# A compression layer with its token windows as the stationary operand: two column halves of TensorE, the sums turned afterwards, and one query moved between the two layers

## The chip, the cores and the metric

The kernel runs on one core of one Trainium2 chip. The metric is device microseconds (us) of that core for one launch. Five engines work side by side, each through its own list of instructions in order: TensorE (PE, with its weight loads PEld), VectorE (DVE), ScalarE (ACT), GpSimd (POOL) and SyncE (SP), which issues the loads from HBM. They wait for one another through semaphores.

## The reference

Two transformer blocks over 256 tokens of width 1024: a first model of two layers (four mixers, a dense and an expert feed-forward), then a second one (a recurrent layer, a feed-forward, a sparse attention layer, a feed-forward). The change touches the attention layer of the second model, in its preparation:

```python
def compress(t, pos_emb, w1, b1, w2, b2):
    n_cmp = (S - CMP_BLOCK) // CMP_STRIDE + 1          # 15
    idx = jnp.arange(n_cmp)[:, None] * CMP_STRIDE + jnp.arange(CMP_BLOCK)[None, :]
    blocks = t[:, idx] + pos_emb[:, None, :]
    blocks = blocks.transpose(0, 1, 3, 2, 4).reshape(B, n_cmp, N_KV_GROUPS, CMP_BLOCK * HEAD_DIM)
    return jax.nn.gelu(blocks @ w1 + b1) @ w2 + b2

k_cmp = compress(k_c, cmp_pos[0], cmp_w1[0], ...)      # then rmsnorm and rope
v_cmp = compress(v_c, cmp_pos[1], cmp_w1[1], ...)
```

There are 15 blocks in each of 4 groups, so 60 rows. The first layer of each of the two compressions takes those 60 rows of 2048 numbers to 256 hidden numbers. The queries of the same attention layer are a projection from 1024 to 1024, cut here into four "queries" of 256 columns.

## The kernel before

All weights pass through one stream of units of 128 x 2048 fp32 numbers (1 MB), numbered in the order of `stages()`. SP loads unit after unit into a ring of four slots (`load`, L765); a slot's next load waits until PE has used the unit that held it, which PE tells by the counter `unit_used`. In the stages around the change the slots follow one another in turn, so unit n + 4 waits for unit n. A "raw" unit is multiplied as it stands, in fp32: each such product is two passes (two matmul records) of PE. Every other unit is split first: ACT copies it rounded (`split`, `high<-ring`, L832), DVE subtracts that from the unit (`low`, `ring_lo<-ring,high`, L2434), and PE makes three single-pass products of the parts (`split_mm`). PE's products all go through the helper line L1409, ACT's instructions through L832.

The stage `keys_and_queries` (L2245 on PE) does in this order: four tiles of keys and two of values, `k_mean`, query 0, query 1, `k_rot` (4 passes of 512 columns), `hidden_layer(0)`, `query_rot(0)` (4 such passes), `hidden_layer(1)`, query 2 with the gates woven in (`gate_step`), the second layer of the key compression (`k_cmp`), query 3 with means, `cmp_mean` and the value compression woven in (`mean_step`, `cmp_step`), `cmp_rot`. The attention follows.

`hidden_layer(v)` (L2167) takes two raw units `cmp`. The weights, 128 x 128 pieces of the unit in `ring`, are the stationary operand; the moving one is the 60 windows in `work` at EXW. Two column tiles m of the hidden layer, each a sum over 16 pieces: 32 products, 64 passes. The result stands with hidden numbers in the partitions, so ACT can add the bias of each hidden number and take the gelu as it evicts (`hidden_layer`, L1323). ACT loads a table before the first gelu. `gate_step` writes the bank from which gelu 0 reads, and so waits for it.

On ACT the order is: eviction of queries 0 and 1, gelu 0, split of the unit of query 2, gelu 1, split of the unit of query 3, `k_copies` (8 copies), eviction of query 2, `k_cmp`, gates, `cmp_norm`. On DVE: the rotation of the keys `k_rope` (L2685 to L2687), `low` of query 2's unit, `query_rope(0)` (the same three lines), `low` of query 3's unit, `cmp_squares`, `cmp_normed`.

Of the kernel before, what the change touches and what calls it, by code (L numbers as in the profile page):

```python
# [25 lines left out]
ACT = mybir.ActivationFunctionType  # L26
AX = mybir.AxisListType.X

P = 128
# [48 lines left out]
def stages():  # L78

    def mixers(l):  # L80
        return [(f"win{l}", NWIN, False), (f"gate_a{l}", 8, False), (f"branch_a{l}", 2, True),
                (f"gate_b{l}", 8, False), (f"branch_b{l}", 2, True), (f"out{l}", NPROJ, False)]

    return [*mixers(0), ("dense", 2 * PART_UNITS, False), *mixers(1), ("moe", NE * PART_UNITS, False),
            ("lru_in", 6, False), ("lru_gate", 1, True), ("lru_last", 2, False), ("out2", NPROJ, True), ("f0", 2 * PART_UNITS, False),
            ("kv", 6, False), ("query_a", 2, False), ("cmp", 4, True), ("query_b", 2, False),
            ("out3", NPROJ, False), ("f1", 2 * PART_UNITS, False)]


# [199 lines left out]
def weight_stream(a):  # L289
# [12 lines left out]
    def narrow(w):  # L302
        for n in range(0, w.shape[1], 256):
            add(rows(w[:, n:n + 256]))
# [55 lines left out]
    for v in range(2):  # L360
        for i in range(2):
            add(rows(a["cmp_w1_2"][v][1024 * i:1024 * i + 1024]))
    narrow(a["b_w_in_2"][0][:, D // 2:D])
    output(a["b_w_out_2"][0])
    ffn(1)
    return np.stack(units)
# [47 lines left out]
def build(nc, stream, consts_in, params_in, x_in, out):  # L414
    units = Units()
    assert units.count == stream.shape[0]
    with ExitStack() as ctx:
# [3 lines left out]
        def sem(name):  # L421
            return ctx.enter_context(nc.semaphore(name))
# [138 lines left out]
        Y_AT, Z_IN, R_AT, GI_AT, A_AT, XR_AT, TH_AT = 0, 2048, 8192, 10240, 12288, 18944, 20992  # L561
        Q_BANK = (6, 7, 4, 5)

        def q_means(i):
            return banks[:, 6 + i, 0:32]

# [45 lines left out]
        def slots_of(a):  # L612
# [27 lines left out]
        kv_out = sem("kv_out")  # L640
        KV_V = Steps(sem("kv_vector"), "windows", "k_squares", "k_normed", "k_rope", "cmp_squares", "cmp_normed",
                     "cmp_rope", "v_cmp")
        KV_P = Steps(sem("kv_products"), "k_mean", "k_rot", "k_cmp", "cmp_mean", "v_cmp", "cmp_rot")
        KV_A = Steps(sem("kv_scalar"), "k_norm", "hidden0", "hidden1", "k_copies", "k_cmp", "cmp_norm")

        Q_P = Steps(sem("q_products"), "rot0", "gates", "mean0", "rot1", "mean1")
        Q_A = Steps(sem("q_scalar"), "input", "out0", "out1", "out2", "gates", "norm0", "out3", "norm1")
# [179 lines left out]
        def _(act):  # L827
# [3 lines left out]
            def f(out_, in_, func, **kw):  # L831
                return act.activation(out_, in_, func, **kw)  # L832
# [442 lines left out]
            def keys_and_queries():  # L1275
# [21 lines left out]
                run(f(w(KSQ, 1024), bank(2, 2), ACT.Sqrt, bias=const("rms_eps")), KV_A, "k_norm")  # L1297
                query(0)
                query(1)
                hidden_layer(0)  # L1300
                split(units.at("query_b"))
                hidden_layer(1)
                split(units.at("query_b", 1))
                act.wait_ge(KV_V.sem, KV_V.at("k_rope"))
                for b in range(2):
                    for d in range(2):
# [3 lines left out]
                query(2)  # L1310
                act.wait_ge(KV_P.sem, KV_P.at("k_cmp"))
                run(f(w(KCM, G * NC), bank(2)[:, 0:G * NC], ACT.Identity, bias=par("cmp_b2k")), KV_A, "k_cmp")
                act.wait_ge(Q_P.sem, Q_P.at("gates"))
                run(f(w(GA, 96), bank(0)[:, 0:96], ACT.Sigmoid), Q_A, "gates")
                act.wait_ge(KV_P.sem, KV_P.at("cmp_mean"))
# [5 lines left out]
                    split(units.at("out3", i))  # L1321

            def hidden_layer(v):  # L1323
                act.wait_ge(unit_used, units.at("cmp", 2 * v + 1) + 1)
                for m in range(2):
                    ins = f(w(HIDN + 128 * v + 64 * m, G * NC), bank(v)[:, 64 * m:64 * m + G * NC],
                            ACT.Gelu_apprx_tanh, bias=par("cmp_b1", 2 * v + m))
                run(ins, KV_A, f"hidden{v}")

            def query_unit(q):  # L1330
                return units.at("query_a", q) if q < 2 else units.at("query_b", q - 2)

            def query(q):
                act.wait_ge(unit_used, query_unit(q) + 1)
                f(w(QSQ + 512 * q, 512), banks[:, Q_BANK[q], :], ACT.Square)
                run(f(w(QR + 512 * q, 512), banks[:, Q_BANK[q], :], ACT.Copy, scale=par("q_norm")), Q_A, f"out{q}")
# [70 lines left out]
        def _(pe):  # L1407
# [758 lines left out]

            def hidden_layer(v):  # L2167

                first = units.at("cmp", 2 * v)
                for i in range(2):  # L2170
                    raw_ready(first + i)
                if v == 0:
                    pe.wait_ge(KV_V.sem, KV_V.at("windows"))
                for m in range(2):
                    for j in range(CB // 2):
                        ins = mm(bank(v)[:, 64 * m:64 * m + G * NC], raw_rows(first + j // 8, 8)[:, j % 8, m * P:m * P + P],
                                 w(EXW + 960 * v + j * G * NC, G * NC), j == 0, j == CB // 2 - 1)
                ins.then_inc(unit_used, 2)

            def query(q):  # L2180

                pe.wait_ge(kv_out, 4 if q < 2 else 6)
                if q == 0:
                    pe.wait_ge(Q_V.sem, Q_V.at("input_lo"))
                g = units.at("query_a", q) if q < 2 else units.at("query_b", q - 2)
                split_ready(g)
                for j in range(2):
                    for k in range(KT):
                        if q == 2:
                            gate_step(KT * j + k)  # L2190
                        elif q == 3:
                            mean_step(0, KT * j + k)
                            cmp_step(KT * j + k)
                        ins = split_mm(banks[:, Q_BANK[q], j * T:j * T + T], parts_of(g, 2 * P * k + j * P, P),
                                       [v[:, k, :] for v in LOWER], k == 0, k == KT - 1)
                ins.then_inc(unit_used, 1)
# [27 lines left out]
            def cmp_step(n):  # L2224

                if n == 4 * TT:
                    pe.wait_ge(KV_V.sem, KV_V.at("cmp_squares"))
                    KV_P.mark(mm(bank(1)[:, 0:G * NC], const("head_mean"), w(EXW, G * NC)), "cmp_mean")
                g = n - 4 * TT - 1
                if 0 <= g < G:  # L2230
                    at, _ = CONSTS["ones"]
                    o = bank(3, rows=slice(0, NC))[:, g * HD:g * HD + HD]
                    for m in range(2):
                        mm(o, w(HIDN + 128 + 64 * m + g * NC, NC), par("cmp_w2v", m * HD, HD), m == 0, False)
                    ins = mm(o, consts[0:1, at:at + NC], par("cmp_b2v", 0, HD, slice(0, 1)), False, True)
                    if g == G - 1:
                        KV_P.mark(ins, "v_cmp")

# [6 lines left out]
            def keys_and_queries():  # L2245
# [14 lines left out]
                KV_P.mark(ins, "k_rot")  # L2260
                hidden_layer(0)
                query_rot(0)
                hidden_layer(1)
                query(2)
                pe.wait_ge(KV_A.sem, KV_A.at("hidden1"))
                pe.wait_ge(KV_V.sem, KV_V.at("k_rope"))
                for m in range(2):
                    ins = mm(bank(2)[:, 0:G * NC], par("cmp_w2k", m * P, P), w(HIDN + 64 * m, G * NC), m == 0, m == 1)
                KV_P.mark(ins, "k_cmp")
                query(3)  # L2270
                pe.wait_ge(KV_V.sem, KV_V.at("cmp_normed"))
                KV_P.mark(mm(bank(2)[:, 0:G * NC], const("swap"), w(KCM, G * NC)), "cmp_rot")
# [144 lines left out]
        def _(dve):  # L2417
# [769 lines left out]
            def keys_and_queries():  # L3187
# [33 lines left out]
                       KV_V, "k_rope")  # L3221
                low(units.at("query_b"))
                query_rope(0)
                low(units.at("query_b", 1))
                dve.wait_ge(KV_A.sem, KV_A.at("k_cmp"))
                k, sq = w(KCM, G * NC), w(EXW, G * NC)
                run(tt(sq, k, k, MUL), KV_V, "cmp_squares")
# [139 lines left out]
```

## Time and profile before

| | |
|---|---|
| median of 3 runs | 1875.35 us (1872.57 to 1876.69) |
| profiled execution: its own time, its span | 1869.12 us, 1867.3 us |
| PE busy, share of the span | 1818.3 us, 97% |
| DVE, ACT busy | 1403.9 us (75%), 1019.7 us (55%) |
| HBM read | 360.39 MB, 194 GB/s over the span |

The profile is of one execution; its span is what the trace covers, and its own time is 1.8 us longer. Starts in the rows are microseconds from the start of the span. A busy PE is not always PE at its peak: its records overlap, so the pace of a stream is read from the distance of starts.

### The profile page before, as it was taken

How to read it: one execution, taken by the hardware profiler on the slowest of the kernel's cores; microseconds unless marked ns; L12 is line 12 of the kernel's file. 1: busy time of each engine (PE TensorE's matmuls, PEld its weight loads, DVE VectorE, ACT ScalarE, POOL GpSimd, SP SyncE). 2: the span in 40 equal slices, each digit the busy share in tenths (PEclk: the TensorE clock that was granted, in tenths of full speed). 3: DMA queues.
4: the chain of work that ended last, by engine and by line, in shares of the span. 5: the costliest groups of instructions: out<-in, count | busy, mean ns of one | idle time of the engine just before them, and what ended most of it. 6: DMA issues, size and time to landing. Idle time of an engine off the chain costs nothing.

```text
span 1867.3 us, 30106 instructions
## 1 busy us (share of the span) xinstructions
PE 1818.3 (97%) x12742; PEld 1577.1 (84%) x12742; DVE 1403.9 (75%) x1540; ACT 1019.7 (55%) x1209; POOL 148.7 (8%) x161
## 2 busy tenths in 40 slices
PE   7999999999999999999999999999999999799999
PEld 7998898888899889788888888895888898578887
DVE  5988667856588966699999999775857564958674
ACT  5663346433566425477777777766533435855431
POOL 0021000201002100000000000000112000001110
PEclk9999999999999999999999999999999999899999
DMA  7432345553443234589999999555553343016451
GB/s 275 158 106 100 113 181 228 186 196 123 168 160 114 92 113 181 194 333 353 350 353 371 350 349 351 192 176 203 188 194 144 143 162 136 1 70 248 169 218 63
DMA packets 52267, 364.49 MB, mean 195 GB/s; under 512 B 5920, under 2 KB 6048, under 8 KB 9760
## 3 DMA queue, kind: packets, MB, share of 16 engines
q1 hardware_dynamic: 50832, 357.79, 51.5%
q0 software_dynamic: 1296, 4.72, 0.7%
q8 instruction: 103, 1.69, 0.4%
q14 instruction: 36, 0.29, 0.0%
HBM read 360.39 MB, written 2.10 MB: 194 GB/s over the span
## 4 chain that ended last, share of the span: by engine, by line
PE 59%; DVE 4%; ACT 2%; issue 1%; DVEq 0%; ACTq 0%
PE banks L1409 57%; ACT work L832 1%; DVE work L3254 1%; DVE small L3258 1%; PE banks L2070 1%; ACT h_parts L832 0%; DVE h_parts L2491 0%; PE banks L2016 0%; PE banks L2316 0%; DVE work L2816 0%; DVE work L2813 0%; DVE more_lo L2434 0%; PE banks L1456 0%; ACT L832 0%; ACT more_high L832 0%
## 5 line engine op out<-in xcount | busy, mean ns | idle before, releaser
L1409 PE MATMUL banks<-h_parts,high 128*128 128x256 f32 (+1 forms) x2576 | 554.0, 307 | 3.3 <-DVE h_parts L2491 2.5
L1409 PE MATMUL banks<-h_parts,ring_lo 128*128 128x256 f32 x1664 | 469.3, 282 | 0.0
L1409 PEld LDWEIGHTS banks<-h_parts,high 128*128 128x128 f32 x2576 | 417.3, 191 | 32.3 <-issue 10.6
L2434 DVE TENSOR_TENSOR ring_lo<-ring,high 128x2048 fp32r<-128x2048 f32 x154 | 352.8, 2299 | 70.1 <-ACT high L832 68.2
L832 ACT ACTIVATE high<-ring 128x2048 fp32r<-128x2048 f32 x154 | 292.4, 1904 | 72.2 <-DMA ring<-weights_in 66.0
L1409 PEld LDWEIGHTS banks<-h_parts,ring_lo 128*128 128x128 f32 x1664 | 317.5, 191 | 0.1
L832 ACT ACTIVATE work<-banks 128x512 f32<-128x512 f32 (+5 forms) x135 | 86.6, 647 | 254.8 <-PE banks L1409 246.9
L2434 DVE TENSOR_TENSOR more_lo<-more,more_high 128x2048 fp32r<-128x2048 f32 (+1 forms) x86 | 188.6, 2203 | 31.9 <-ACT more_high L832 31.8
L1409 PE MATMUL banks<-h_parts,more_high 128*128 128x512 f32 x592 | 207.6, 394 | 2.0 <-DVE more_lo L2434 1.5
L832 ACT ACTIVATE more_high<-more 128x2048 fp32r<-128x2048 f32 (+1 forms) x86 | 158.0, 1842 | 61.7 <-DMA more<-weights_in 61.5
L832 ACT ACTIVATE glu<-scr 128x256 f32<-128x256 f32 x66 | 27.6, 419 | 219.9 <-DVE scr L2458 219.9
L1409 PE MATMUL banks<-more_high,h_parts 128*128 128x512 f32 (+1 forms) x440 | 138.1, 384 | 0.1
L2455 DVE TENSOR_REDUCE scr<-banks 128x512 f32<-128x1024 f32 x66 | 80.8, 1224 | 75.2 <-PE banks L1409 75.2
L1409 PE MATMUL banks<-high,h_parts 128*128 128x256 f32 (+1 forms) x520 | 135.9, 343 | 0.0
L1409 PEld LDWEIGHTS banks<-h_parts,more_high 128*128 128x128 f32 x592 | 111.1, 188 | 27.8 <-DVE more_lo L2434 2.1
L2434 DVE TENSOR_TENSOR ring_lo<-ring,more_high 128x2048 fp32r<-128x2048 f32 (+1 forms) x60 | 133.5, 2226 | 0.2
L1409 PE MATMUL banks<-h_parts,more_lo 128*128 128x256 f32 x448 | 125.2, 280 | 0.0
L832 ACT ACTIVATE more_high<-ring 128x2048 fp32r<-128x2048 f32 (+1 forms) x60 | 111.3, 1856 | 24.3 <-DMA ring<-weights_in 24.2
L1409 PE MATMUL banks<-work 32*32 32x32 f32 (+8 forms) x2592 | 119.0, 237 | 5.1 <-DVE work L2743 2.4
L1409 PE MATMUL banks<-more_high,g_hi 128*128 128x512 f32 x294 | 115.9, 394 | 0.0
L1409 PEld LDWEIGHTS banks<-work 32*32 32x32 f32 (+5 forms) x2592 | 94.1, 132 | 25.3 <-issue 15.4
L1409 PE MATMUL banks<-more_high,g_lo 128*128 128x512 f32 x294 | 115.0, 391 | 0.0
(283 smaller groups left out, 3076.4 us busy)
## 6 DMA issues: line engine op xcount, KB each, us to landing
ring<-weights_in SPq DMA_DIRECT2D x225, 1024.0 KB, 4.9
more<-weights_in SPq DMA_DIRECT2D x104, 1024.0 KB, 5.2
more<-weights_in SPq DMA_DIRECT2D x8, 512.0 KB, 4.0
ring<-weights_in SPq DMA_DIRECT2D x6, 512.0 KB, 3.8
consts<-consts_in SPq DMA_DIRECT2D x1, 2034.0 KB, 17.4
params<-params_in SPq DMA_DIRECT2D x1, 1162.5 KB, 11.1
x<-x_in SPq DMA_DIRECT2D x2, 512.0 KB, 4.1
normed_rows<-scr POOLq DMA_DIRECT2D x2, 512.0 KB, 10.3
```

The costliest lines, as they stand in the source:

```text
L832: return act.activation(out_, in_, func, **kw)
L1409: return pe.matmul(out_, lhsT, rhs, start=start, stop=stop, **kw)
L2070: ins = pe.transpose(bank(2 + s % 2)[:, c * P:c * P + P], token_hidden[:, s % 2, c * P:c * P + P], const("ident"))
L2434: tt(lo_of(g), ring_of(g), hi_of(g).bitcast(F32), SUB).then_inc(unit_lo, 1)
L2455: chain.to(dve.tensor_reduce(ffn_sum(t), pair, AX, ADD), sums_made, done)
L3254: ins = tt(s[:, 2 * r:2 * r + 2, :], grid(bank(2 * (k % 2) + r)[:, 0:2 * n], 2), bc(mask, 2), ADD)
L3258: run(dve.tensor_reduce(least, s, AX, MAX, negate=True))
```

## The change

The first layer is turned round: the 60 windows become the stationary operand and the 128 x 128 weight pieces the moving one. The two tiles m are written to partitions 0 to 59 and 64 to 123 of one bank, in turn, so each uses one half of PE's columns. The sums now stand with windows in the partitions; ACT copies them to `work`, PE turns them with two transposes (`hidden_turn`), and ACT takes the gelu as before. The stage list becomes cmp0, query_b (query 2), cmp1, query_c (query 3): the first layer of the values and its turn come behind query 2 and `k_cmp`, the turn inside query 3. `unit_used` is now raised after each unit of the layer, not by two at its end.

```diff
-            ("kv", 6, False), ("query_a", 2, False), ("cmp", 4, True), ("query_b", 2, False),
+            ("kv", 6, False), ("query_a", 2, False), ("cmp0", 2, True), ("query_b", 1, False),
+            ("cmp1", 2, True), ("query_c", 1, False),
...
# ACT, keys_and_queries
                 query(0)
                 query(1)
+                split(units.at("query_b"))
                 hidden_layer(0)
-                split(units.at("query_b"))
-                hidden_layer(1)
-                split(units.at("query_b", 1))
                 act.wait_ge(KV_V.sem, KV_V.at("k_rope"))
...
                 query(2)
                 act.wait_ge(KV_P.sem, KV_P.at("k_cmp"))
                 run(f(w(KCM, G * NC), bank(2)[:, 0:G * NC], ACT.Identity, bias=par("cmp_b2k")), KV_A, "k_cmp")
+                split(units.at("query_c"))
+                hidden_layer(1)
...
             def hidden_layer(v):
-                act.wait_ge(unit_used, units.at("cmp", 2 * v + 1) + 1)
+                act.wait_ge(unit_used, units.at(f"cmp{v}", 1) + 1)
                 for m in range(2):
-                    ins = f(w(HIDN + 128 * v + 64 * m, G * NC), bank(v)[:, 64 * m:64 * m + G * NC],
+                    ins = f(w(EXW + 960 * v, P, rows=window_rows(m)), bank(v, rows=window_rows(m))[:, 0:P], ACT.Copy)
+                run(ins, KV_A, f"sums{v}")
+                act.wait_ge(KV_P.sem, KV_P.at(f"turned{v}"))
+                for m in range(2):
+                    ins = f(w(HIDN + 128 * v + 64 * m, G * NC), bank((v + m) % 2)[:, P + 64 * m:P + 64 * m + G * NC],
                             ACT.Gelu_apprx_tanh, bias=par("cmp_b1", 2 * v + m))
# PE
             def hidden_layer(v):
-                first = units.at("cmp", 2 * v)
-                for i in range(2):
-                    raw_ready(first + i)
+                first = units.at(f"cmp{v}")
                 if v == 0:
                     pe.wait_ge(KV_V.sem, KV_V.at("windows"))
+                for j in range(CB // 2):
+                    if j % 8 == 0:
+                        raw_ready(first + j // 8)
+                    for m in range(2):
+                        ins = mm(bank(v, rows=window_rows(m))[:, 0:P], w(EXW + 960 * v + j * G * NC, G * NC),
+                                 raw_rows(first + j // 8, 8)[:, j % 8, m * P:m * P + P], j == 0, j == CB // 2 - 1)
+                    if j % 8 == 7:
+                        ins.then_inc(unit_used, 1)
+
+            def hidden_turn(v):
+
+                pe.wait_ge(KV_A.sem, KV_A.at(f"sums{v}"))
                 for m in range(2):
-                    for j in range(CB // 2):
-                        ins = mm(bank(v)[:, 64 * m:64 * m + G * NC], raw_rows(first + j // 8, 8)[:, j % 8, m * P:m * P + P],
-                                 w(EXW + 960 * v + j * G * NC, G * NC), j == 0, j == CB // 2 - 1)
-                ins.then_inc(unit_used, 2)
+                    ins = pe.transpose(bank((v + m) % 2)[:, P + 64 * m:P + 64 * m + G * NC], w(EXW + 960 * v, P, rows=window_rows(m)),
+                                       const("ident")[window_rows(m), 64 * m:64 * m + G * NC])
+                KV_P.mark(ins, f"turned{v}")
...
# PE, query(q)
                     for k in range(KT):
+                        if q == 3 and KT * j + k == 2:
+                            hidden_turn(1)
...
# PE, cmp_step
                 if n == 4 * TT:
+                    pe.wait_ge(KV_A.sem, KV_A.at("hidden1"))
...
# PE, keys_and_queries
                 hidden_layer(0)
                 query_rot(0)
-                hidden_layer(1)
+                hidden_turn(0)
                 query(2)
-                pe.wait_ge(KV_A.sem, KV_A.at("hidden1"))
                 pe.wait_ge(KV_V.sem, KV_V.at("k_rope"))
                 for m in range(2):
                     ins = mm(bank(2)[:, 0:G * NC], par("cmp_w2k", m * P, P), w(HIDN + 64 * m, G * NC), m == 0, m == 1)
                 KV_P.mark(ins, "k_cmp")
+                hidden_layer(1)
                 query(3)
```

What PE does from `k_rot` (the first row) to the first step of query 2, before (one row is one instruction of the program, xN of them):

```order
L1409 MATMUL banks<-work,consts 128x512 x2
L1409 MATMUL banks<-work,ring 128x60 x32
L1409 MATMUL banks<-work,consts 128x512 x2
L1409 MATMUL banks<-work,ring 128x60 x32
L1409 MATMUL banks<-params,work 128x48
L1409 MATMUL banks<-hb_hi,high 128x256
```

And in the changed kernel (`params,work 128x48` is the first gate step of query 2):

```order
L1420 MATMUL banks<-work,consts 128x512 x2
L1420 MATMUL banks<-ring,work 60x128 x32
L1420 MATMUL banks<-work,consts 128x512 x2
L2196 MATMUL banks<-consts,work 128x60 x2
L1420 MATMUL banks<-params,work 128x48
L1420 MATMUL banks<-hb_hi,high 128x256
```

The second layer has left this place, and the two transposes of the first one's sums stand directly ahead of query 2.

What ACT does from the eviction of query 1 on, before:

```order
L832 ACTIVATE work<-banks,params 128x512
L832 ACT_TABLE_LOAD
L832 ACTIVATE work<-banks,params 128x60 x2
L832 ACTIVATE high<-ring 128x2048
L832 ACTIVATE work<-banks,params 128x60 x2
L832 ACTIVATE high<-ring 128x2048
L832 ACTIVATE work<-work 64x2x256 x8
L832 ACTIVATE work<-banks 128x512
L832 ACTIVATE work<-banks,params 128x512
L832 ACTIVATE work<-banks,params 128x60
L832 ACT_TABLE_LOAD
```

And in the changed kernel:

```order
L839 ACTIVATE work<-banks,params 128x512
L839 ACTIVATE high<-ring 128x2048
L839 ACTIVATE work<-banks 60x128 x2
L839 ACT_TABLE_LOAD
L839 ACTIVATE work<-banks,params 128x60 x2
L839 ACTIVATE work<-work 64x2x256 x8
L839 ACTIVATE work<-banks 128x512
L839 ACTIVATE work<-banks,params 128x512
L839 ACTIVATE work<-banks,params 128x60
L839 ACTIVATE high<-ring 128x2048
L839 ACTIVATE work<-banks 60x128 x2
L839 ACTIVATE work<-banks,params 128x60 x2
```

The split of query 2's unit (the first `high<-ring`) moved ahead of the first gelu, which now has two copies and the transposes ahead of it, with its table load behind the wait for the transposes. The split of query 3's unit (the second `high<-ring`) moved from ahead of the eight copies of `k_copies` to behind the eviction of query 2 and `k_cmp`.

DVE and SP have the same rows in the same order as before; the units that they take are renumbered.

## Rows read from the trace of the kernel before

**Rows 1.** The page: busy time of engines, and the clock that PE was granted.

```profile
PE 1818.3 (97%) x12742; PEld 1577.1 (84%) x12742; DVE 1403.9 (75%) x1540; ACT 1019.7 (55%) x1209; POOL 148.7 (8%) x161
...
PEclk9999999999999999999999999999999999899999
```

**Rows 2.** Timeline of PE around the layers: start, duration, operation, passes, idle before.

```profile
1532.00 1.88 PE L1409 MATMUL banks<-work,consts 128*128 128x512 f32 x4
1533.71 7.25 PE L1409 MATMUL banks<-work,ring 128*128 128x60 f32 x64
1540.80 1.94 PE L1409 MATMUL banks<-work,consts 128*128 128x512 f32 x4
1542.58 7.25 PE L1409 MATMUL banks<-work,ring 128*128 128x60 f32 x64
1550.25 0.39 PE L1409 MATMUL banks<-params,work 128*128 128x48 f32 x2 [0.42 <-issue]
...
1560.48 0.55 PE L1409 MATMUL banks<-work,params 128*128 128x60 f32 x4
1560.87 0.34 PE L1409 MATMUL banks<-consts,work 128*128 128x2 f32 x2
...
1571.56 0.33 PE L1409 MATMUL banks<-work,consts 128*128 128x60 f32 x2
```

**Rows 3.** Weight loads of PE, 1515 to 1572, then 1572 to 1660, by form.

```profile
L1409 PEld LDWEIGHTS banks<-work,ring 128*128 128x128 f32 x128 | 14.6, 192 | 1.0 <-issue 1.0
...
L1409 PEld LDWEIGHTS banks<-work 128*64 128x64 f32 x192 | 10.8, 143 | 2.9 <-issue 2.9
```

**Rows 4.** Timeline of PE in the attention: transposes, sums in two column halves.

```profile
1638.48 0.63 PE L2316 MATMUL banks<-consts,work 128*128 128x128 f32 x4 [0.61 <-ACT work L832]
1639.04 2.85 PE L1409 MATMUL banks<-work 15*64 15x128 f32 x40
1641.81 0.61 PE L2310 MATMUL banks<-consts,work 128*15 128x128 f32 x4
...
1645.07 1.09 PE L2316 MATMUL banks<-consts,work 128*128 128x128 f32 x8 [2.03 <-ACT work L832]
1646.09 3.20 PE L1409 MATMUL banks<-work 15*64 15x128 f32 x24
```

**Rows 5.** Windows in that stream: length, busy and passes touched per engine, clock.

```profile
1639.55:1639.65 0.10, 0.10 (x4) 0.10 (x4) 0.10 (x1) 0.10 (x1) 0.00 (x0) 1.00 0.00 0
1639.55:1640.20 0.65, 0.65 (x14) 0.65 (x14) 0.61 (x2) 0.65 (x3) 0.00 (x0) 1.00 0.00 0
```

**Rows 6.** Timeline of ACT, first a norm's evictions, then this stage.

```profile
1480.10 4.22 ACT L832 ACTIVATE h_parts<-banks,params 128x128 fp32r<-128x128 f32 x16
...
1532.75 0.68 ACT L832 ACTIVATE work<-banks,params 128x512 f32<-128x512 f32 x1
1541.05 1.28 ACT L832 ACT_TABLE_LOAD   x1 [7.61 <-PE banks L1409]
1542.34 0.51 ACT L832 ACTIVATE work<-banks,params 128x60 f32<-128x60 f32 x2
1545.84 1.91 ACT L832 ACTIVATE high<-ring 128x2048 fp32r<-128x2048 f32 x1 [2.99 <-issue]
...
1552.23 5.11 ACT L832 ACTIVATE work<-work 64x512 f32<-64x512 f32 x8
1560.74 0.60 ACT L832 ACTIVATE work<-banks 128x512 f32<-128x512 f32 x1 [3.40 <-PE banks L1409]
1561.35 1.03 ACT L832 ACTIVATE work<-banks,params 128x512 f32<-128x512 f32 x2
...
1565.97 1.28 ACT L832 ACT_TABLE_LOAD   x1 [2.03 <-PE banks L1409]
```

**Rows 7.** Timeline of DVE in this stage.

```profile
1533.98 1.22 DVE L2685 TENSOR_TENSOR work<-banks,consts 128x1024 f32<-128x1024 f32 x1 [4.09 <-PE banks L1409]
...
1536.50 1.23 DVE L2687 TENSOR_TENSOR work<-work 128x1024 f32<-128x1024 f32 x1
1547.86 2.29 DVE L2434 TENSOR_TENSOR ring_lo<-ring,high 128x2048 fp32r<-128x2048 f32 x1 [10.13 <-ACT high L832]
...
1568.24 0.28 DVE L3230 SCALAR_TENSOR_TENSOR work<-work,params 128x60 f32<-128x60 f32 x1
```

**Rows 8.** SP's loads L765, 1525 to 1545: issues and time to landing.

```profile
L765 SPq DMA_DIRECT2D ring<-weights_in x4: 328/328/431, 1526.4 to 1541.4; - x4
...
DMA to landing us min/median/max: 4.8/4.8/6.9
```

**Rows 9.** Windows of all engines (PE first, then PEld, DVE, ACT, POOL), clock.

```profile
1578.10:1605.30 27.20, 17.80 (x110) 14.09 (x110) 23.88 (x55) 20.14 (x52) 0.00 (x0) 0.50 0.00 1
...
1643.10:1645.00 1.90, 0.00 (x0) 0.00 (x0) 1.61 (x5) 1.90 (x7) 0.00 (x0) 1.00 0.00 0
1646.40:1653.10 6.70, 6.70 (x40) 5.14 (x37) 5.21 (x4) 4.11 (x5) 0.00 (x0) 0.50 0.00 1
1258.60:1260.20 1.60, 0.00 (x0) 0.00 (x0) 1.57 (x3) 1.55 (x4) 0.00 (x0) 1.00 0.64 102
1261.00:1270.00 9.00, 9.00 (x24) 4.37 (x23) 3.27 (x4) 8.18 (x14) 0.00 (x0) 1.00 0.18 76
```

More of the change, by code:

```diff
@@ L362, in weight_stream @@
             add(rows(a["cmp_w1_2"][v][1024 * i:1024 * i + 1024]))
-    narrow(a["b_w_in_2"][0][:, D // 2:D])
+        narrow(a["b_w_in_2"][0][:, D // 2 + 256 * v:D // 2 + 256 * v + 256])
     output(a["b_w_out_2"][0])
@@ L562, in build, with window_rows @@
         Q_BANK = (6, 7, 4, 5)
+        def window_rows(m):
+            return slice(64 * m, 64 * m + G * NC)
         def q_means(i):
@@ L642, in build @@
                      "cmp_rope", "v_cmp")
-        KV_P = Steps(sem("kv_products"), "k_mean", "k_rot", "k_cmp", "cmp_mean", "v_cmp", "cmp_rot")
-        KV_A = Steps(sem("kv_scalar"), "k_norm", "hidden0", "hidden1", "k_copies", "k_cmp", "cmp_norm")
+        KV_P = Steps(sem("kv_products"), "k_mean", "k_rot", "turned0", "k_cmp", "turned1", "cmp_mean", "v_cmp", "cmp_rot")
+        KV_A = Steps(sem("kv_scalar"), "k_norm", "sums0", "hidden0", "k_copies", "k_cmp", "sums1", "hidden1",
+                     "cmp_norm")
         Q_P = Steps(sem("q_products"), "rot0", "gates", "mean0", "rot1", "mean1")
@@ L1330, in query_unit @@
             def query_unit(q):
-                return units.at("query_a", q) if q < 2 else units.at("query_b", q - 2)
+                return units.at("query_a", q) if q < 2 else units.at(("query_b", "query_c")[q - 2])
             def query(q):
@@ L2184, in query @@
                     pe.wait_ge(Q_V.sem, Q_V.at("input_lo"))
-                g = units.at("query_a", q) if q < 2 else units.at("query_b", q - 2)
+                g = units.at("query_a", q) if q < 2 else units.at(("query_b", "query_c")[q - 2])
                 split_ready(g)
@@ L3223, in keys_and_queries @@
                 query_rope(0)
-                low(units.at("query_b", 1))
+                low(units.at("query_c"))
                 dve.wait_ge(KV_A.sem, KV_A.at("k_cmp"))
```

## The prediction

> **What bounds the kernel now.** The page comes first [rows 1]. PE is busy for 1818.3 of 1867.3 us, 97%, and at the full granted clock but for one slice of forty. So a microsecond less of PE work is a microsecond less of time, as long as PE doesn't wait in its place. The second view is PE's timeline around the two layers [rows 2]. Each layer is 64 passes of 60 moving columns. The first lasts from 1533.71 to 1540.80, 7.09 us or 111 ns a pass; the second from 1542.58, with a tail and a wait of 0.42 us, to query 2 at 1550.25: 7.67 us. Between them stand the four passes of `query_rot(0)`, and the four of `k_rot` with the same shape take 1.71 us (1532.00 to 1533.71). A 512-column fp32 pass thus has a pace of 427 ns, or 0.83 ns a column; 60 columns would be 50 ns. The layer's 111 ns are therefore not the moving columns, and the other thing that each pass has is a full load of 128 x 128 weights [rows 3].
>
> **The layer turned round.** The trace holds the same form in the attention: `at_sum` multiplies with 64 stationary columns, 128 moving ones, and its two results go to partitions 0 to 63 and 64 to 127 in turn. One such block of 40 passes goes from 1639.04 to 1641.81, 69 ns a pass [rows 4]. In its inside a window of 0.10 us touches 4 passes and one that is 0.55 us longer touches 14: 55 ns a pass [rows 5]. By the pace above a pass of 128 columns alone would be 107 ns, so the two halves run together. The stationary load of 64 columns shows 143 ns against 192 for 128 [rows 3]. I take 55 ns, since the layer is one unbroken alternation of 64 passes: 3.5 us. 69 ns is the dearer neighbour (4.4 us). The far end is that nothing is gained by the halves, 111 ns as today.
>
> What lies between 55 and 69 is the change of form: 40 passes at 55 ns are 2.2 us, and the other 0.57 us falls on five changes between stationary pieces of 15 and 128 rows and into and out of the block, 0.11 us each. That is what I put beside every change here: into and out of the layer 0.22 us, so 3.72 us for a layer. The Trainium skill (TensorEngine Tiling (Array Packing), Tiling Modes) has the rule that speaks against this change: changing the tiling mode, not just the tile, drains TensorE. The trace agrees, with 0.11 us a change; that rule without a price would leave the layer at 3.5 us.
>
> **From the first layer to query 2.** Before: 1533.71 to 1550.25, 16.54 us [rows 2]. After: layer 3.72, `query_rot(0)` 1.71, transposes. Four transposes of `at_turn` stand 0.56 us apart from the next work (1638.48 to 1639.04) [rows 4], so two cost 0.28 us, with a change 0.39. Sum 5.82 us, at 1539.5. The copies of the sums on ACT are covered: ACT starts 0.26 us after PE goes on (1560.48, 1560.74), and 16 evictions of 128 columns took 4.22 us, 0.26 each [rows 2, 6], so they are done at 1537.4 + 0.26 + 0.53 = 1538.2, a little under 1 us before `query_rot(0)` ends. Without that cover they would cost 0.8 us.
>
> The gelu isn't covered. Query 2 begins with a gate step into the bank from which the gelu reads. Before, ACT did its table load and two gelus (1541.05 to 1542.85, 1.80 us) [rows 6] while PE worked on the second layer; that layer has now gone behind query 2. So PE waits for 0.26 us to reach ACT, 1.80 us, and about 0.07 us back: **2.13 us** of new wait. Query 2 starts 5.82 + 2.13 = 7.95 us after the layer's start, at 1541.7, against 16.54: a lead of 8.6 us. The wait of 0.42 us is in this lead. Its cause was the load of query 2's unit, issued when the first layer had freed its slot (SP's last issue of this stretch is at 1541.4 [rows 8]), then ACT's split at 1545.84 and DVE's `low` until 1550.15 [rows 6, 7]. Now that unit takes the slot that query 0 frees: issue at 1526.4, landing 4.8 to 6.9 us later, by 1533.3 [rows 8]. ACT splits it after query 1's eviction (done 1533.4), DVE takes its low part after `k_rope` (done 1537.7) [rows 6, 7], so it is there at 1540.1, 1.6 us ahead. Cmp1's units come into slots freed at 1532 and halfway through the first layer, and query 3's at its end: all are in the ring by 1545, before use.
>
> **From query 2 to query 3.** Query 2 itself stays 10.23 us (1550.25 to 1560.48), and I count from its end, T = 1551.9. Before, query 3 began at T + 0.39, behind `k_cmp` [rows 2]. Now PE does `k_cmp` and the second layer, 0.39 + 3.72 = 4.1 us. But the split of query 3's unit was moved on ACT behind the eviction of query 2 and `k_cmp`. That chain: 0.26 us to ACT, eviction with `k_cmp` 1.64 (1560.74 to 1562.38), split 1.92, 0.1 to DVE, `low` 2.29, 0.1 to PE [rows 6, 7]: T + 6.31. So PE waits **2.2 us** more, with its second layer hidden inside the chain whatever its price up to 5.9 us. ACT meanwhile stands idle for some 5 us between `k_copies` (5.11 us, done near 1546.9) and T + 0.26; the queue order alone keeps the split out of there. The loss against T + 0.39 is 5.92 us.
>
> **In query 3.** Two transposes with two changes: 0.28 + 0.22 = 0.50 us. The second layer's gelu has no table load and must be done at step 8 of 16, some 3 us later. The table loads for gates and `cmp_norm` and the DVE work follow `cmp_mean` in that step. Before, they ended at 1568.5 (from ACT's 1565.97), 3 us ahead of `cmp_rot` at 1571.56 [rows 2, 6, 7], and that distance stays. Nothing is late next; the attention starts when query 3 ends.
>
> **The sum.** 8.6 - 5.92 - 0.50 = 2.2 us less. Counted the other way: 7.09 + 7.67 go; 2 x 3.72 + 0.39 + 0.50 + 2.13 + 2.2 = 12.66 come; 2.1 us. The profiled execution has a span of 1867.3 us and its own time of 1869.12, so this one would be near 1866.9. It lies 6.2 us under the median of 1875.35, for no reason that a row shows, and I take the difference to the median: **1873.1 us**, 0.12% less. A measurement of this kernel tells a difference from about 0.2%, 3.8 us; most of the saving of 6.9 us on the layers is spent on two waits.
>
> **Rivals.**
> - *The halves are dearer than in `at_sum`.* At 69 ns a pass the first layer is 0.7 to 0.9 us longer and the second stays hidden: gain 1.4, 1873.9. At 111 ns the first costs 3.6 more and the second ends at T + 7.7, 1.4 after the chain: 2.8 us slower, 1878.2. For it: 60 columns are not 64, and the moving side comes from the ring. Against it: load, columns and alternation are the same form. Chance 0.10, nearly all of it within 0.2%.
> - *The clock falls in the new waits.* PE was held at 0.50 for 27.3 us from 1578.1, and for 6.8 us after the idle time of 2.03 us at 1643.04 and eight transposes [rows 4, 9]. There 24 passes of the halves took 3.13 us, 130 ns each instead of 69 [rows 4]. The changed kernel has waits of 2.1 and 2.2 us, one just behind transposes. Against it: around the 1.70 us of idle time at 1258.5, between dense work, the clock stayed at 1.00 [rows 9], and here too dense products lie on both sides. A stretch of 6.8 us at half the clock costs 3.4 us: one makes 1876.5, one behind each wait 1879.9, slower by 4.6 us. It decides above 12 us at the low clock in this stage. Chance 0.15, about half of it slower by over 0.2%.
> - *The attention's slow stretch moves.* It runs at 1.2 GHz for 27.3 us with PE busy for 17.8 of 27.2 [rows 9]. If it begins later or ends earlier by a quarter, that is 17.8 / 4 / 2 = 2.2 us, and with the gain of the layers 4.4: 1870.9. It can go the other way as well. Chance 0.15.
> - *The waits don't show*, because gate steps or the split are let through earlier than the order has them: up to 2.2 + 4.3 = 6.5 us, 1868.8. Against it: both waits are semaphores that the moved instructions raise. Chance 0.05.
>
> **How the numbers follow.** My forecast, a gain of 1 to 3.5 us, has 0.55. Range 1868.8 to 1878.6: from the last rival, through the spread of the shown runs (1872.6 to 1876.7, shifted by 2.2), to between one and two stretches at the low clock; its two ends leave some 0.1 each. Faster by over 0.2%: most of the third and fourth rivals and the forecast's edge, 0.23. Slower: 0.11. Within: 0.66.
>
> **What would show it.** In the changed profile the 64 passes of a layer, 60 stationary and 128 moving columns, go by in 3.5 to 3.8 us; PE has an idle time of about 2.1 us ahead of query 2, ended by ACT's gelu, and one of about 2.2 us ahead of query 3, ended by DVE's `low`; ACT is idle for 5 us between `k_copies` and the eviction of query 2; from the start of the first layer to `cmp_rot` 35.6 us pass, before 37.85. I am wrong if the first layer has a pace near 70 or 110 ns, if either wait is missing or longer, or if the granted clock falls between 1539 and 1570.

## The result, and the profile after

| | before | changed |
|---|---|---|
| median of 6 runs each | 1873.96 us (1870.96 to 1876.69) | 1880.76 us (1870.71 to 1883.69) |
| the profiled execution | 1869.12 us | 1870.71 us |
| its mean granted clock | 0.991 | 0.989 |

The ratio is 1.0038, with a 95% interval of 1.002 to 1.0057: slower by a little, 6.8 us at the medians. The forecast was 1873.1 us in a range to 1878.6. The profile of the changed kernel is of its fastest execution; the other five took 1878.8 to 1883.7 us at a mean clock of 0.981 to 0.984.

PE's timeline shows every planned piece at nearly its planned size (start, duration, passes, idle before; compare [rows 2]):

```profile
1534.14 3.71 PE L1420 MATMUL banks<-ring,work 128*60 128x128 f32 x64
1537.78 1.98 PE L1420 MATMUL banks<-work,consts 128*128 128x512 f32 x4
1539.70 0.27 PE L2196 MATMUL banks<-consts,work 60*128 60x60 f32 x2
1542.01 0.39 PE L1420 MATMUL banks<-params,work 128*128 128x48 f32 x2 [2.04 <-ACT work L839]
...
1552.24 0.55 PE L1420 MATMUL banks<-work,params 128*128 128x60 f32 x4
1552.72 3.71 PE L1420 MATMUL banks<-ring,work 128*60 128x128 f32 x64
1558.58 0.35 PE L1420 MATMUL banks<-consts,work 128*128 128x2 f32 x2 [2.15 <-issue]
...
1575.98 0.52 PE L1420 MATMUL banks<-work,consts 128*128 128x60 f32 x2
```

A layer takes 3.64 us from start to start (3.72 forecast), 57 ns a pass; query 2 begins 7.87 us after the layer (7.95), behind an idle time of 2.04 us (2.13); query 3 begins 6.34 us after query 2's end (6.31), behind 2.15 us (2.2). At query 3's start the changed kernel is 2.7 us ahead, counted from the first layer. Then query 3 takes 17.4 us to `cmp_rot` at 1575.98, where 11.2 were forecast. ACT's timeline has the cause of the second wait, the split behind 5.48 us of idle time and query 2's eviction; DVE's `low` hangs on that split:

```profile
1541.90 5.12 ACT L839 ACTIVATE work<-work 64x512 f32<-64x512 f32 x8
1552.50 0.60 ACT L839 ACTIVATE work<-banks 128x512 f32<-128x512 f32 x1 [5.48 <-PE banks L1420]
1553.11 1.03 ACT L839 ACTIVATE work<-banks,params 128x512 f32<-128x512 f32 x2
1554.17 1.91 ACT L839 ACTIVATE high<-ring 128x2048 fp32r<-128x2048 f32 x1
...
1556.18 2.29 DVE L2457 TENSOR_TENSOR ring_lo<-ring,high 128x2048 fp32r<-128x2048 f32 x1 [12.14 <-ACT high L839]
```

The view puts PE's second wait down to "issue", but `low` ends at 1558.47, 0.11 us before query 3 starts, so it is what PE waited for.

Why query 3 is slow stands in the windows (engines as in [rows 9], the granted clock behind POOL):

```profile
1558.60:1561.00 2.40, 2.40 (x20) 2.20 (x21) 0.01 (x1) 0.71 (x3) 0.00 (x0) 1.00 0.96 294
1561.10:1578.10 17.00, 17.00 (x84) 14.19 (x84) 2.60 (x9) 4.29 (x7) 0.00 (x0) 0.50 0.12 41
1578.20:1588.30 10.10, 9.31 (x108) 7.86 (x106) 9.41 (x16) 6.64 (x5) 0.00 (x0) 1.00 0.22 91
1588.50:1608.80 20.30, 9.62 (x46) 6.66 (x48) 18.43 (x46) 15.20 (x51) 0.00 (x0) 0.50 0.01 1
```

About 2.5 us into query 3 the clock falls from 2.4 to 1.2 GHz and stays there for 17 us with PE busy all the time. It then comes back for 10 us, just for the part of the attention that ran at the low clock before. These are PE's rows there, two of the kernel before (L1409, L2316) and two of the changed one:

```profile
1576.64 10.28 PE L1409 MATMUL banks<-work 64*128 64x128 f32 x88
1592.04 1.11 PE L2316 MATMUL banks<-consts,work 128*128 128x128 f32 x4 [5.12 <-DVE work L3271]
...
1581.44 6.07 PE L1420 MATMUL banks<-work 64*128 64x128 f32 x88
1594.90 1.11 PE L2339 MATMUL banks<-consts,work 128*128 128x128 f32 x4 [7.39 <-DVE work L3294]
```

The 88 passes take 6.1 us instead of 10.3, but PE then waits 2.3 us longer for DVE, so from `cmp_rot` to these transposes only 1.6 us are won (18.92 against 20.48). Another 1.3 us come back near 1650, where the low stretch lasts 3.4 us instead of 6.8. So of the 4.0 us that the stage is longer (41.84 against 37.85) the attention gives back 2.9 in this execution. The 10 us at the full clock stand in all four profiles with a long fall in query 3 (below), so they aren't what makes this execution the fastest of its kernel; what the slower ones do differently this profile can't show.

### The profile page after: what moved, and what is told of

Its sections match the earlier page's. It is cut to its first block, busy times and chain, and to the rows that moved or that the text cites. A ratio compares the mean times of both kernels' runs of the same rounds, so it can differ in the third digit from the quotient of the medians.

```text
span 1868.9 us, 30119 instructions
## 1 busy us (share of the span) xinstructions
PE 1814.0 (97%) x12746; PEld 1570.7 (84%) x12746; DVE 1403.6 (75%) x1540; ACT 1020.7 (55%) x1213; POOL 148.9 (8%) x161
## 4 chain that ended last, share of the span: by engine, by line
PE 58%; DVE 5%; ACT 2%; issue 1%; DVEq 0%; ACTq 0%
PE banks L1420 57%; DVE work L3277 1%; DVE small L3281 1%; ACT work L839 1%; PE banks L2081 1%; ACT h_parts L839 0%; DVE h_parts L2514 0%; PE banks L2027 0%; DVE work L2839 0%; PE banks L2339 0%; DVE work L2836 0%; DVE more_lo L2457 0%; DVE ring_lo L2457 0%; ACT L839 0%; PE banks L1467 0%
## 5 line engine op out<-in xcount | busy, mean ns | idle before, releaser
L839 ACT ACTIVATE work<-banks 128x512 f32<-128x512 f32 (+6 forms) x139 | 87.8, 637 | 259.7 <-PE banks L1420 252.5
L1420 PE MATMUL banks<-work 32*32 32x32 f32 (+8 forms) x2592 | 115.1, 233 | 5.0 <-DVE work L2766 2.7
## 6 DMA issues: line engine op xcount, KB each, us to landing
normed_rows<-scr POOLq DMA_DIRECT2D x2, 512.0 KB, 10.2
```

The costliest lines, as they stand in the source:

```text
L1420: return pe.matmul(out_, lhsT, rhs, start=start, stop=stop, **kw)
```

## The experiments

Each run lists the mean granted clock c of every execution. The time at the low clock (1.2 GHz, half of the full one) is then 2 x (1 - c) x time, good to some 2 us for the rounding of c. Through the executions of one kernel the time rises by 0.35 to 0.43 us for each microsecond at the low clock (straight lines through the three sets of the kernel before, and through 12 executions of the changed one), so a time less 0.39 times its low time is an estimate of what that execution would take at the full clock. The profile has the same price: query 3 loses 6.2 us in 17 at the low clock, 0.36 for each. The last two columns are medians over the executions. A difference in the last column hangs on the slope where the low times differ much: at 0.36 the changed kernel gains 0.9 us, at 0.43 it gains 2.6. The runs came in three groups, each with its own runs of the kernel before on the same chip.

| kernel | runs | median us | ratio to before (95%) | low clock, us | less 0.39 x low |
|---|---|---|---|---|---|
| before, group 1 | 35 | 1871.0 | | 37 | 1857 |
| changed again | 12 | 1879.0 | 1.0039 (1.0025 to 1.0052) | 58 | 1855.5 |
| both waits filled | 12 | 1870.2 | 0.9993 (0.9982 to 1.0004) | 39 | 1855 |
| second wait only | 12 | 1875.3 | 1.0016 (1.0002 to 1.0029) | 56 | 1854.5 |
| neither wait | 12 | 1866.6 | 0.9973 (0.9961 to 0.9985) | 41 | 1851 |
| before, group 2 | 31 | 1873.6 | | 41 | 1857.5 |
| before with a wait | 11 | 1879.9 | 1.003 (1.0013 to 1.0048) | 56 | 1859 |
| first wait only | 9 | 1868.2 | 0.9966 (0.9936 to 0.9996) | 41 | 1854 |
| new order, old form | 12 | 1871.5 | 0.9985 (0.9973 to 0.9996) | 37 | 1857 |
| new form, old order | 12 | 1871.8 | 0.9986 (0.9973 to 0.9999) | 49 | 1853.5 |
| before, group 3 | 30 | 1872.8 | | 39 | 1857 |
| means in the wait | 12 | 1870.3 | 0.9996 (0.9982 to 1.0011) | 45 | 1853 |
| second wait filled | 12 | 1870.2 | 0.9988 (0.9975 to 1.0) | 37 | 1855 |
| neither wait, again | 12 | 1864.5 | 0.9957 (0.9944 to 0.9971) | 32 | 1851 |
| the same, attention's gap filled | 7 | 1864.5 | 0.9957 (0.9941 to 0.9973) | 26 | 1853.5 |

### The changed kernel again

> The changed kernel once more, to see how its executions spread and whether their time goes with the time at the low clock. Theory 1 (the waits ahead of query 2 and query 3 let the clock fall, in most executions already ahead of query 3 or at query 2): executions with a mean clock near 0.983 take about 1880 us, those near 0.989 about 1871 us; the profile has a stretch at 0.50 that begins between 1543 and 1562. Theory 2 (the added time is something else, such as loads or the chip's other noise): times between 1871 and 1884 us without relation to the mean clock.

1879.0 us, 8 above the kernel before. The time goes with the clock: from 1872.5 us at 0.988 to 1883.7 at 0.981. The windows of its profile:

```profile
1541.70:1543.60 1.90, 0.00 (x0) 0.00 (x0) 1.87 (x3) 1.84 (x4) 0.00 (x0) 1.00 0.94 358
1545.30:1548.60 3.30, 3.30 (x17) 3.30 (x17) 0.40 (x1) 3.24 (x6) 0.00 (x0) 0.50 0.01 2
1548.70:1559.60 10.90, 10.90 (x124) 10.44 (x123) 0.18 (x1) 3.51 (x4) 0.00 (x0) 1.00 0.25 90
1559.70:1561.80 2.10, 0.00 (x0) 0.02 (x1) 2.10 (x2) 0.54 (x2) 0.00 (x0) 1.00 1.01 402
1562.40:1582.70 20.30, 20.30 (x100) 17.17 (x100) 2.39 (x9) 5.08 (x9) 0.00 (x0) 0.50 0.16 55
```

Both waits are followed by a fall here. The one behind the first wait lasts 3.4 us, the one behind the second over 20 us. Theory 1 holds; the spread is that of the clock. This execution is at 0.986, so the median one (0.984) isn't profiled either.

### Both waits filled

```diff
+                if q == 2:
+                    keep_busy(4, 4)
+                elif q == 3:
+                    keep_busy(5, 4)
                 split_ready(g)
```

`keep_busy(b, n)` makes n products of constants of 256 columns into bank b, here free until the query writes it.

> Each of the two waits is filled with 4 products of constants into a free bank (8 passes of 256 fp32 columns, about 1.7 us of the 2.0 and 2.2 us of idle time); nothing of them is used. The waits themselves stay. Theory 1 (idle time lets the clock fall): the clock stays at 1.00 until the attention, the stage takes about 35.6 us, the median is about 2 us under the kernel before, near 1872. Theory 2 (the form of the layer, 60 stationary columns in halves, is what lets the clock fall): as the changed kernel, near 1880, with a fall before 1562.

PE's timeline at the two places, and the windows from there:

```profile
1541.71 0.27 PE L2196 MATMUL banks<-consts,work 60*128 60x60 f32 x2
1541.91 2.00 PE L1420 MATMUL banks<-consts 128*128 128x256 f32 x8
...
1558.37 1.99 PE L1420 MATMUL banks<-consts 128*128 128x256 f32 x8
1560.54 0.38 PE L1420 MATMUL banks<-consts,work 128*128 128x2 f32 x2 [0.17 <-DVE ring_lo L2461]
```

```profile
1560.50:1571.50 11.00, 10.96 (x91) 9.37 (x92) 1.35 (x5) 3.91 (x7) 0.00 (x0) 1.00 0.33 122
```

Query 3 still begins at the same distance from query 2, and still waits for DVE, but it runs at the full clock. The stage takes 35.5 us (1536.15 to 1571.68), where the forecast had 35.6. The time is 8.8 us under the changed kernel, with the same order, layer form and waits. So what costs is that PE is idle in the waits, and the halves and transposes are cleared. The median is 1.8 us lower than expected, at the same low time as before.

### Second wait only, first wait only

The first wait is taken away by turning the first layer's sums into banks 5 and 1, which the gate steps don't touch, and by waiting for the gelu ahead of `k_cmp`:

```diff
+        TURNED = ((5, 1), (1, 0))
...
-                if n == 0:
-                    pe.wait_ge(KV_A.sem, KV_A.at("hidden0"))
...
                 query(2)
+                pe.wait_ge(KV_A.sem, KV_A.at("hidden0"))
```

> The turned sums of the first layer go to banks 5 and 1, so the gate steps need not wait for the gelu; the wait for it stands ahead of k_cmp. The first wait (2.04 us) is gone, the second stays. Theory 1 with either wait sufficient: the clock still falls behind the second, near 1561, the median between 1874 and 1880. If the first wait is the one that decides (or both are needed): about 4 us under before, near 1870. Query 2 starts about 2 us earlier either way.

1875.3 us. Query 2 begins after 0.56 us of idle time (it now waits for DVE's low part of its unit), the second wait is 2.15 us, and the clock falls behind it: 17 us at 0.50 from 1562.6 in the profile. The time at the low clock is 56 us, close to the changed kernel's 58. Eight of the 12 executions are at a mean clock of 0.984 to 0.986, four at 0.988 to 0.992.

The second wait is taken away by the place of one line on ACT:

```diff
                 run(ins, KV_A, "k_copies")
+                split(units.at("query_c"))
                 query(2)
...
-                split(units.at("query_c"))
                 hidden_layer(1)
```

> The changed kernel with the split of query 3's unit moved on ACT to directly behind k_copies: the second wait (2.15 us) goes, the first (2.04 us, ahead of query 2) stays. Together with the run that had only the second wait it shows which of the two costs the clock. Theory 1a (either wait alone is enough): time at the low clock near that of the run with the second wait alone, median near 1874. Theory 1b (the first wait costs at most a short stretch, as in the profile that showed 3.4 us behind it): the time is that of the sum, 4.4 us under before, 1867 to 1869.

1868.2 us, a ratio of 0.9966. The first wait stands in the profile with 2.04 us of idle time, and the clock is 1.00 from there to `cmp_rot`. Only one of nine executions was at a mean clock under 0.989 (0.982, 1881.7 us). Theory 1b: the loss at the low clock hangs on the second wait. The first one still costs time by itself: at an equal clock this kernel takes 3 us more than the one with neither wait (1854 against 1851), whose stage is 1.5 us shorter in the profiles (31.87 against 33.36).

### Only the second wait filled

> The changed kernel with only the second wait filled, by 4 products of constants (8 passes of 256 columns, 1.7 us). The first wait is left. If the second wait alone makes the loss: as with both filled, about 1 us under the kernel before, no additional time at the low clock. If the first matters too: between that and the changed kernel.

The edit is the second half of that of both fillings. 1870.2 us and 37 us at the low clock, as with both filled. Its profile has a fall of 3.4 us behind the first wait (the first window), and none behind the second until the attention:

```profile
1543.70:1546.90 3.20, 3.20 (x17) 3.20 (x16) 0.31 (x1) 3.14 (x6) 0.00 (x0) 0.50 0.01 3
1558.00:1577.50 19.50, 18.82 (x152) 15.43 (x152) 8.78 (x17) 6.63 (x13) 0.00 (x0) 1.00 0.44 164
```

So the first wait is followed by a short stretch in some executions (two of the five profiles that have this wait unfilled), too little to be seen in the median. Stretches of 3.4 us stand at places without such a wait too, near 675 us in three of the 14 profiles.

### The kernel before with a wait

```diff
                 KV_P.mark(ins, "k_cmp")
+                pe.wait_ge(KV_V.sem, KV_V.at("cmp_squares"))
                 query(3)
```

> The kernel before with one wait added: PE waits ahead of query 3 until DVE has made the squares of the compressed keys (about 1.9 us of idle time; nothing else is changed, no halves, no turns, old order). Theory 1 (idle time of about 2 us ahead of query 3 lets the clock fall, whatever the form of the layer): about 15 to 20 us more at the low clock than the kernel before in most executions, the median 1.9 + 6 to 8 us above it, near 1880. Theory 2 (the fall also needs what the changed kernel does around the wait, the halves or the transposes): only the wait itself, about 1.9 us, 1873.

PE's timeline and the windows behind it, of a kernel with the old form and the old order:

```profile
1564.32 0.55 PE L1409 MATMUL banks<-work,params 128*128 128x60 f32 x4
1566.53 0.38 PE L1409 MATMUL banks<-consts,work 128*128 128x2 f32 x2 [1.66 <-DVE work L3228]
```

```profile
1566.60:1568.80 2.20, 2.20 (x19) 2.20 (x20) 0.00 (x0) 1.17 (x2) 0.00 (x0) 1.00 0.88 372
1568.90:1585.80 16.90, 16.90 (x83) 13.86 (x83) 2.82 (x10) 3.04 (x5) 0.00 (x0) 0.50 0.05 13
```

An idle time of 1.66 us makes the kernel before 6.2 us slower, with 15 us more at the low clock; at an equal clock 1.5 to 2 us of this are left, which is the wait itself. So the fall comes without anything else of the change, and the second theory is ruled out. Over all profiles: in the four that have a wait of 1.7 to 2.2 us ahead of query 3 the clock falls 0.5 to 2.5 us after query 3 starts, and in the other ten it doesn't fall in query 3.

### New order with the old form, new form in the old order

The first has the old `hidden_layer` on PE and ACT (64 passes of 60 columns, no turn) in the changed kernel's order. The second has the halves and turns, with cmp0, cmp1, query 2, query 3 in the order of before, the first layer's sums turned into banks 5 and 4, and the gates waiting for the second gelu.

> The new order (second layer and query 3's split behind query 2) with the old form of the layer: weights stationary, 60 moving columns, no copies of sums, no transposes. The layer is 7.1 us again, so it covers ACT's and DVE's chain ahead of query 3, and most of the gelu ahead of query 2 (0.4 us of wait left). By the sum the stage is 0.2 us shorter than before: median within 1 us of the kernel before, no additional time at the low clock. If the order itself costs something, it shows here.

Layers of 7.08 us, no idle time above 0.3 us, the stage 37.24 us (1536.20 to 1573.44), 0.6 less than before; 2.2 us less at the median, more than the 1 us expected, and 0.8 at an equal clock. The order by itself is no loss; while the layer is long, it covers the waits.

> The new form of the layer (60 stationary columns in two halves, sums turned) in the old order: both layers ahead of query 2. PE saves the same 6.9 us, but query 2's unit is loaded only when the first layer has freed its slot: issue near 1536, landed 4.8 us later, split 1.9, low part 2.3, so PE waits about 4 us ahead of query 2, and the stage is about 2.9 us shorter than before at an equal clock. Theory 1 (waits of 2 us and more let the clock fall): the clock falls at query 2, the median is above before. Without a fall: 1868.

The stage is 33.5 us (1537.83 to 1571.33), shorter than the 35.0 I expected, since the second layer's wait for its sums (0.70 us) and that for query 2's unit (1.73 us) are in the place of one of 4 us. That is 2.1 us shorter than the changed kernel's sum. The median gains 1.9 us, neither the loss of Theory 1 nor the 1868 without a fall; at an equal clock it would be 4. The waits stand ahead of query 2. The median time at the low clock is 8 us above that of before, but the means are 44 and 43 us, and the profile, of an execution at 0.992, has no fall in the stage. So it isn't shown that these waits cost clock.

### The means in the wait

```diff
+                if q == 3:
+                    for n in range(4 * TT):
+                        mean_step(0, n)
                 split_ready(g)
...
-                            mean_step(0, KT * j + k)
```

> The changed kernel, but the 8 mean products of query 3 (16 passes of 2 moving columns under full weight loads, some 0.11 us each) stand ahead of the wait for its unit instead of between its products. They fill 1.8 of the 2.15 us of the second wait with narrow passes and make query 3 1.7 us shorter. At an equal clock 3.5 to 4 us under the kernel before. Theory 1 (what counts is that PE isn't idle): no fall, median near 1868. Theory 2 (narrow passes count for as little as idle time, and it is query 3's narrow passes beside the wait that keep the clock low): the fall is still there, about 20 us more at the low clock than before, median 1874 to 1877.

The 16 narrow passes fill the wait (1557.53 on, no idle time above 0.3 us behind them), and the profile has the full clock to `cmp_rot`. Ten of 12 executions are at 0.987 to 0.991, two at 0.984 and 0.985. The median is only 2.5 us under before and the interval holds 1, though at an equal clock 4 us are gained. With this wait filled by wide products all but one of 12 executions were at 0.988 to 0.993. The run doesn't settle whether the narrow passes do as well.

### Neither wait

The two edits of "Second wait only, first wait only" together; the second run is the same kernel again.

> As the last one, and the split of query 3's unit stands on ACT directly behind k_copies, where ACT was idle for 5 us. Both waits of PE are gone. Theory 1: no fall of the clock before the attention; from the first layer to cmp_rot about 31.5 us instead of 37.85, the median 5 to 6.5 us under before, near 1868. Theory 2 (the form of the layer lets the clock fall): a stretch at the low clock begins before 1562 all the same, and the time is above 1872.

> The kernel without the two waits (turned sums in other banks, query 3's split directly behind k_copies) once more, for a tighter interval: 4.4 to 6.2 us under the kernel before, a ratio of 0.997 to 0.9975.

1866.6 and 1864.5 us, 4.4 and 8.3 under the kernel before of the same group. The second is more than the 6.2 expected at most, with 9 us less at the low clock than the first; at an equal clock both gain 6 us. PE's timeline of the second run:

```profile
1534.90 3.71 PE L1421 MATMUL banks<-ring,work 128*60 128x128 f32 x64
1538.55 1.98 PE L1421 MATMUL banks<-work,consts 128*128 128x512 f32 x4
1540.46 0.28 PE L2197 MATMUL banks<-consts,work 60*128 60x60 f32 x2
1541.30 0.39 PE L1421 MATMUL banks<-params,work 128*128 128x48 f32 x2 [0.56 <-DVE ring_lo L2457]
...
1552.00 3.71 PE L1421 MATMUL banks<-ring,work 128*60 128x128 f32 x64
1555.64 0.38 PE L1421 MATMUL banks<-consts,work 128*128 128x2 f32 x2
...
1566.77 0.33 PE L1421 MATMUL banks<-work,consts 128*128 128x60 f32 x2
```

The stage takes 31.87 us instead of 37.85, with one idle time of 0.56 us. This is the gain of the new form and order without the two waits, and it is faster than both kernels.

### The attention's gap filled

> The same, with 6 products of constants (12 passes of 256 columns, 2.6 us at the full clock, 5.1 at half of it) into a free bank in PE's idle time of 5 us ahead of the first transposes of the attention. If the clock returns earlier from the stretch at 0.50 that holds for 20 to 30 us there, 2 to 4 us less than without; if it stays low whatever is in that gap, no difference or up to 0.5 us more.

`keep_busy(4, 6)` stands behind the last compressed scores. In the profile the low clock holds for 6.8 and 10.2 us there instead of 30.7, and the mean clock rises to 0.993. The median is the same 1864.5 us, not the 2 to 4 us less that an earlier return of the clock was expected to bring. Part of this stretch PE spends waiting for DVE (next row), where a faster clock wins nothing, and the filling takes PE's time (4.20 us for 12 passes):

```profile
1580.73 4.28 PE L1421 MATMUL banks<-consts 128*128 128x256 f32 x12
1584.93 1.13 PE L1421 MATMUL banks<-work 64*128 64x256 f32 x8
1587.81 0.66 PE L2339 MATMUL banks<-consts,work 128*128 128x128 f32 x4 [1.74 <-DVE work L3295]
```

How much each of the two takes was not told apart.

## Why the prediction was wrong

**Right, with the measured sizes.** What bounds the kernel; the price of the halves (57 ns a pass against 55, read from `at_sum`); 0.09 us for entering the form at the second layer (1552.24 to 1552.72 is 0.48 for `k_cmp` with the change, 0.39 without), against 0.11; the transposes (both under 0.3 us, without the changes of form beside them); both waits, their size, place and releaser; ACT's idle time of 5 us. With both waits filled the stage takes 35.5 us, where the forecast had 35.6. At an equal clock the changed kernel is an estimated 1.7 us faster, where the sum had 2.2. The low part of query 2's unit is there 6.25 us after the first layer's start, 6.4 in the sum; with the gelu's wait gone it is what PE waits for next, 0.56 us. The Trainium skill (TensorEngine Tiling (Array Packing), Tiling Modes) has it that a change of tiling mode drains TensorE; the trace agrees in so far as the entry costs these 0.09 us.

**The step that failed.** The sum had no term for the clock: it priced the two waits at their own length, 2.13 and 2.2 us. What it left out stood in the rival "The clock falls in the new waits", given 0.15 and priced at 3.4 us a stretch of 6.8 us, so that only two of them would be slower by over 0.2%. What I held against it was the idle time of 1.70 us at 1258.5 between dense work with the clock at 1.00 [rows 9]. Behind that one stands work of another kind:

```profile
1260.24 1.56 PE L1409 MATMUL banks<-consts 128*128 128x256 f32 x6 [1.70 <-ACT work L832]
1261.64 20.76 PE L1409 MATMUL banks<-ring,work 128*128 128x512 f32 x48
```

Six passes of constants (the kernel before has `keep_busy` at five places already) and 48 unbroken passes of 512 columns are not query 3 with its narrow products, so it was no like neighbour, though no run tells whether this is what counts. The runs show that a wait of 1.66 us ahead of query 3 is enough in most executions, and the stretch behind it is 17 to 20 us in each of the four profiles that have that wait unfilled (the changed kernel twice, the one with the second wait only, the kernel before with a wait). At half the clock query 3 takes 17.4 us and not 11.2. The median pays 21 us more at the low clock, 0.39 us for each: 8.2 us, less the gain of 1.7, is 6.5, and 6.8 and 8.0 were measured. I had rows for the length as well, 27.3 us in the attention [rows 9], and took the shorter neighbour. The 6.2 us between the profiled execution and the median, "for no reason that a row shows", are in part clock as well: the shorter times of that kernel go with the higher mean clocks. And the median of three from which the forecast was counted, 1875.35 us, lay higher than any later one of the kernel before (1871.0 to 1873.6 us over 96 executions). The rival "The attention's slow stretch moves" came true beside it: 20.5 us instead of 27.3 in both profiles of the changed kernel, with 1.6 us won there in the first, where 2.2 was priced.

**What stays open.** Why the wait ahead of query 2, 2.04 us long, is followed by 3.4 us or nothing at the low clock, and that of 1.66 to 2.15 us ahead of query 3 by 17 to 20 us. What differs in the rows is what follows: gate steps of 48 columns in query 2, mean products of 2 columns in query 3. With the means moved into the wait there was no long fall in the profile, but idle time went as well, so the two aren't told apart. No profile caught an execution of the changed kernel at its median clock or below (0.984 to 0.981). The two profiled ones have 44 and 54 us at the low clock in all; where the further time lies isn't shown.

## What to carry to other kernels

Price a wait on a dense PE at the clock that follows it, not at its own length: here 1.7 to 2.1 us of idle time at one place cost 6 to 8 us, and idle time of 2.0 us at another place, 17 us earlier, cost no clock that could be measured, only some 1.5 to 3 us for itself. When a piece of PE work is made shorter, look first for what it had been covering, and move that (here one `split` line and one bank) in the same change; the change as it stood was a loss of 0.4% and with the cover mended a gain of 0.27% to 0.43%. When executions spread, set their times against the mean granted clock before explaining them: one straight line separated the kernel's own gain of about 2 us from the clock's 8.

## What the hardware showed that I had not expected

- PE can be busy for 17 to 20 us at the low clock without it coming back, in a stretch of 256-column products with narrow ones between (0.50 from 1561.1 to 1578.1).
- 1.66 us of idle time is enough to bring this about. The idle time of 1.7 us near 1258 is followed by no fall in any of the 14 profiles, and that of 2.04 us ahead of query 2 by 3.4 us at 0.50 in two of five.
- Products of constants that nothing reads, put into the two waits, took 8.8 us off the changed kernel.
- Two column halves of 60 stationary columns run at 57 ns a pass of 128 fp32 columns, half of what the 512-column passes give for that width; the weight load in that form shows 133 ns instead of 192:

```profile
L1420 PEld LDWEIGHTS banks<-ring,work 128*60 128x60 f32 x128 | 6.9, 133 | 0.8 <-issue 0.8
```
